# A two-block transformer kernel: the value weights of the dilated attention split over 768 of their 1024 columns, one of their splits issued earlier, and the last two head results read ahead of the keys

## The reference, cut to what matters

```python
proj = h @ w_in                       # 3*768 attention columns, then RWKV-7 streams and gates
y_attn = dilated_attention(proj[..., :2304], positions) @ attn_w_up   # 12 heads of 64, 3 dilations
y_rwkv = rwkv7_time_mix(token_shift(proj[..., 2304:...], mu), ...)
merged = gates[..., :D] * y_attn + gates[..., D:] * y_rwkv
```

## Time and profile before

| what | value |
|---|---|
| runs | 1980.54, 1982.11, 1982.14 us |
| the profiled execution, its own time | 1982.24 us |
| its span in the trace | 1980.4 us |
| PE, ACT, DVE, POOL busy | 96%, 57%, 59%, 39% |
| chain that ended last | 90% PE, 5% DVE, 3% ACT, 1% POOL |

### The profile page before, as it was taken

One profiled execution on the slowest core, in us unless ns is written; L12 is line 12 of the kernel. 1 busy time (PEld: TensorE's weight loads), 2 busy tenths in 40 slices (PEclk: granted clock), 3 DMA queues, 4 the chain that ended last, 5 costly groups with the idle time before them and its releaser, 6 DMA issues.

```text
span 1980.4 us, 33174 instructions
## 1 busy us (share of the span) xinstructions
PE 1909.9 (96%) x12988; PEld 1649.7 (83%) x12988; DVE 1162.0 (59%) x1595; ACT 1133.7 (57%) x1532; POOL 779.5 (39%) x348
## 2 busy tenths in 40 slices
PE   7999989999999999999999999999989899999997
PEld 7999878888987899989787888888878788888885
DVE  2222474766553222264124888888864688888886
ACT  4344556444454544443454777777754467777775
POOL 6888686520068788867772000000057300000000
PEclk9999999999999999999999999999999999999999
DMA  6555443310035555445446998888644579889882
GB/s 233 185 189 186 149 143 138 107 66 3 3 108 186 191 191 190 175 144 192 149 169 260 345 346 341 337 339 340 254 150 158 194 300 343 336 339 345 335 338 98
DMA packets 59315, 425.70 MB, mean 215 GB/s; under 512 B 6577, under 2 KB 7089, under 8 KB 8113
## 3 DMA queue, kind: packets, MB, share of 16 engines
q1 hardware_dynamic: 58032, 419.02, 56.7%
q10 hardware_dynamic: 1152, 4.85, 0.7%
HBM read 422.79 MB, written 1.05 MB: 214 GB/s over the span
## 4 chain that ended last, share of the span: by engine, by line
PE 90%; DVE 5%; ACT 3%; issue 1%; POOL 1%; DMA 0%; SPq 0%; ACTq 0%; DVEq 0%; POOLq 0%
PE ps L735 22%; PE ps L761 19%; PE ps L1319 11%; PE ps L1278 7%; PE ps L1280 7%; PE ps L1279 7%; PE ps L1014 7%; PE ps L1266 2%; PE ps L1333 2%; POOL w_low L692 1%; PE ps L1301 1%; ACT w_high L1507 1%; PE ps L923 1%; PE ps L836 0%; ACT arena L1531 0%
## 5 line engine op out<-in xcount | busy, mean ns | idle before, releaser
L692 POOL TENSOR_TENSOR w_low<-ring,w_high 128x1024 fp32r<-128x1024 f32 x312 | 768.8, 2474 | 671.7 <-ACT w_high L1507 670.8
L1507 ACT ACTIVATE w_high<-ring 128x1024 fp32r<-128x1024 f32 x480 | 504.0, 1060 | 465.5 <-PE ps L761 204.3
L2479 DVE TENSOR_TENSOR w_low<-arena,w_high 128x1024 fp32r<-128x1024 f32 x312 | 373.3, 1222 | 48.7 <-ACT w_high L1507 45.5
L735 PE MATMUL ps<-x_high,w_high 128*128 128x256 f32 x1272 | 365.7, 287 | 6.5 <-DVE x_low L2005 5.1
L1507 ACT ACTIVATE w_high<-arena 128x1024 fp32r<-128x1024 f32 x312 | 323.6, 1059 | 66.0 <-PE ps L1280 49.3
L735 PE MATMUL ps<-x_low,w_high 128*128 128x256 f32 x1272 | 359.8, 283 | 0.0
L735 PE MATMUL ps<-x_high,w_low 128*128 128x256 f32 x1272 | 359.8, 283 | 0.0
L1278 PE MATMUL ps<-w_high,x_high 128*128 128x512 f32 x640 | 256.7, 401 | 3.3 <-DVE x_low L2561 2.8
L735 PEld LDWEIGHTS ps<-x_high,w_high 128*128 128x128 f32 x1272 | 243.8, 192 | 10.7 <-issue 7.9
L1280 PE MATMUL ps<-w_high,x_low 128*128 128x512 f32 x640 | 249.6, 390 | 0.0
L1279 PE MATMUL ps<-w_low,x_high 128*128 128x512 f32 x640 | 248.9, 389 | 0.0
(11 more groups left out here) (312 smaller groups left out, 2361.5 us busy)
## 6 DMA issues: line engine op xcount, KB each, us to landing
ring<-in_stream SPq DMA_DIRECT2D x240, 1024.0 KB, 4.8
arena<-in_stream SPq DMA_DIRECT2D x156, 1024.0 KB, 5.3
arena<-in_gains ACTq DMA_DIRECT2D x4, 512.0 KB, 4.0
con<-in_consts ACTq DMA_DIRECT2D x1, 1280.0 KB, 7.3
con<-in_consts SPq DMA_DIRECT2D x1, 1248.0 KB, 13.8
x<-in_x SPq DMA_DIRECT2D x2, 512.0 KB, 4.0
arena<-in_gate_bias ACTq DMA_DIRECT2D x1, 1024.0 KB, 4.3
out_dram<-arena SPq DMA_DIRECT2D x2, 512.0 KB, 2.6
```

What stands on the lines that cost most here:

```text
L692: nc.gpsimd.tensor_tensor(w_low[:, t % AHEAD, :], slot(SLOT[t // 2])[:, t % 2 * TW:t % 2 * TW + TW], w_high[:, t % AHEAD, :].bitcast(F32), ...
L735: mm = pe.matmul(dst, wp[rows, t % AHEAD, w], xp[rows, x0 + k, :], start=(k == 0 and n == 0), stop=(k == k_tiles - 1 and n == 2))
L1507: nc.scalar.activation(w_high[:, t % AHEAD, :], slot(SLOT[c])[:, t % 2 * TW:t % 2 * TW + TW], ACT.Copy)\
L2479: nc.vector.tensor_tensor(w_low[:, t % AHEAD, :], slot(SLOT[c])[:, t % 2 * TW:t % 2 * TW + TW], w_high[:, t % AHEAD, :].bitcast(F32), ALU. ...
```

## The change

Three edits. First, `columns(t)` gives 768 for the tiles 84 to 91 and 1024 for all others; ACT's split and POOL's subtraction use it, so that the zero padding of the value tiles isn't split. POOL's loop has one width per turn, so its turns 1 to 9 become a loop of six turns, twelve tiles written out (84 to 95, the first eight narrow), and a loop of two turns. Second, the split of tile 87 is issued on ACT after two of the eight key instructions at L1640 instead of after all eight. Third, in the steps 8 and 9 DVE's `evacuate` stands ahead of `keys`, no longer last.

```diff
+        def columns(t):
+
+            return AQ if 2 * START["dil_v"] <= t < 2 * START["dil_v"] + 8 else TW
...
@@ POOL, low(t, turn) @@
-                nc.gpsimd.tensor_tensor(w_low[:, t % AHEAD, :], slot(SLOT[t // 2])[:, t % 2 * TW:t % 2 * TW + TW],
-                                        w_high[:, t % AHEAD, :].bitcast(F32), ALU.subtract).then_inc(w_low_ready, 1)
+                w = columns(t) if turn is None else TW
+                nc.gpsimd.tensor_tensor(w_low[:, t % AHEAD, 0:w], slot(SLOT[t // 2])[:, t % 2 * TW:t % 2 * TW + w],
+                                        w_high[:, t % AHEAD, 0:w].bitcast(F32), ALU.subtract).then_inc(w_low_ready, 1)
...
-            with pool.Fori(1, before_solve) as i:
+            narrow = 2 * START["dil_v"] // 12
+            assert narrow * 12 == 2 * START["dil_v"]
+            with pool.Fori(1, narrow) as i:
+                for t in range(12):
+                    low(t, i)
+            for t in range(narrow * 12, narrow * 12 + 12):
+                low(t)
+            with pool.Fori(narrow + 1, before_solve) as i:
                 for t in range(12):
                     low(t, i)
...
@@ ACT, split(t, turn) @@
-                nc.scalar.activation(w_high[:, t % AHEAD, :], slot(SLOT[c])[:, t % 2 * TW:t % 2 * TW + TW], ACT.Copy)\
+                w = columns(t)
+                nc.scalar.activation(w_high[:, t % AHEAD, 0:w], slot(SLOT[c])[:, t % 2 * TW:t % 2 * TW + w], ACT.Copy)\
                     .then_inc(w_high_ready, 1)
...
@@ ACT, the key instructions at L1640 @@
                     if p == 2:
                         used(t0 + 18)
+                        split_to(t0 + 18 + AHEAD)
...
@@ DVE, the steps n @@
+                    if n >= 8 and n <= 9:
+                        evacuate(n - 2)
                     if n == 5:
                         inverse()
                     if 6 <= n <= 9:
                         keys(n - 6)
                     if n < 8:
                         normalised(n)
-                    if 2 <= n <= 9:
+                    if 2 <= n <= 7:
                         evacuate(n - 2)
```

## The result

The changed kernel takes 1980.9 us (median of 20 runs, 1974.5 to 1985.3) against 1985.3 us for the kernel before (20 runs, 1980.0 to 1992.4): ratio 0.9977, 95% interval 0.9966 to 0.9987, so 4.4 us faster, between 2.6 and 6.7. Forecast were 1975.0 us, in a range of 1972.8 to 1978.4, and 7.2 us of gain. The direction is right. The forecast is 5.9 us too low: by 3.1 because the kernel before is slower than its first three runs said (1982.1, now 1985.3), and by 2.8 because the gain is smaller.

What follows compares the result with a forecast made beforehand. PE, busy 96% of the span, was taken as the bound, so only its idle or low-clock time could be won. 4.5 + 3.6 - 0.1 = 8.0 us, or 6.5 with one fall; 7.2 taken, giving 1975.0 us, range 1972.8 to 1978.4.

Steps and rivals of the forecast that it cites:

- The narrow split: Value tiles 84 to 91: POOL's subtraction 1.82 us for 2.37, scores 4.5 us earlier, 1.5 of it from the clock.
- The early split: ACT's split of tile 87 issued earlier: costed at nothing, bounds 0 to 0.3 us gained, no loss.
- POOL's cut loop: POOL's loop cut in three, seams before tile 84 and at tile 96: taken as 0.
- The head results ahead of the keys: Steps 8 and 9: 2.25 us of PE idle and 1.34 of lower clock saved, 3.6 us.
- The give-back in step 10: L2114's second half might meet a POOL tile, costing PE up to 0.5 us; taken as 0.1.
- The price of the clock: PE's falls to about half clock after idle stretches: each costs about 1.5 us; none or one would remain.
- The level: Starting time of the kernel before: profiled execution 1982.24 us, median 1982.11, so 1982.2 was taken.
- POOL's tile 86 ahead of the sum: Value tiles: POOL's tile 86 starts before DVE's running sum; 1974.7 us, or 1976.2 with a fall; 25%.
- the first rival: Only part arrives: the clock falls twice as before but elsewhere; 5.0 us gained, 1977.1 us; 14%.
- The chances: Odds against a 0.2% (4 us) line: faster 0.84, same 0.13, slower 0.03.

Runs made afterwards that it cites:

- the waits filled: The kernel before with matmuls whose results nobody reads added in PE's three idle stretches; ratios 0.9998 and 1.0001 against the kernel before.
- the fourth measurement: The changed kernel without the early split of tile 87, counted as one more measurement of the same work; ratio 0.9967 (0.9953 to 0.9981) against the kernel before.

## Why the prediction was wrong, point by point

- *The narrow split.* Right. 1.82 us a tile, and 0.85 for ACT's split (0.83 said). From the first value tile to tile 86 it gained 0.5 us, as said (and 0.2 before it), from there to tile 90 2.2 (2.3 said), and from tile 90 to the scores the 1.5 us of the fall, in this pair of profiles.
- *The early split and POOL's cut loop.* Right at nothing: 126.3 us with and without the one, and no gap at either seam.
- *The head results ahead of the keys.* Right: `widen(3)` ended at 375.5 and PE lost 0.2 us there. PE reaches unit 7's result 2.3 us sooner. The give-back in step 10 was put at 0.1 us with a bound of 0.5; it is 0.5, by the mechanism named. The reason given for the low end, "since it met none before", says nothing of the new place: the edit moves that instruction (L2114, now L2128), and the prediction has no time for POOL's tile there.
- *The price of the clock: the term that failed in the gain.* "After 0.7 us of idle PE I expect no fall of the clock, so 1.5 us more" and "1.34 (2.79 - 1.45) of the lower clock" took both falls of one execution as a property of the kernel (and the second is 1.3: at full clock the head result takes 1.50 us). Of the 7.2 us forecast, 2.0 were clock (2.8 if no fall stays, 1.3 if one does) and 5.2 work. The work came: 130.9 - 126.3 = 4.6 us, plus 0.2 ahead of the stretch, so 4.8, and what lacks is the 0.5 us in step 10 that was put at 0.1. The clock didn't: three profiles show the stretch at 133.6, 130.9 and 132.5 us, and 130.9 with the waits filled, so on average 1.4 us and not 2.8. A fall that stands where another engine paces PE costs little or nothing. Work and clock by the profiles make 6.2 us; the runs say 4.8 within 1.4, or 5.2 within 1.3 with the fourth measurement. Whether the last 1 us is chance stays open.
- *The level: the larger error in the time.* "The profiled execution took 1982.24 us ...; the median is 1982.11, so the two stand together." They did, but three runs within 1.6 us of one another came from the fast end of a spread of 12 us. That was bad luck, and three runs couldn't show it. The median of 20 is 1985.3. The range allowed "0.8 for the spread of the runs".
- *The rivals.* POOL's tile 86 ahead of the sum didn't happen, by 0.01 us in the profile after, and in no other profile of the changed kernel (POOL's subtraction takes 6.00 us in all, and PE's first wait is 2.5 us). So near a tie, that it didn't happen is luck as much as reckoning. Of the rest, the first rival had the right size, 5.0 us, and half the reason: less won from the clock. It had the falls only move, which two of the three profiles of the changed kernel don't show: they have none before 400 us.
- *The chances.* The gain lies at the line of 0.2%: 0.23%, with 0.13 to 0.34. 0.84 for clearly faster was too sure.

## What to carry to other kernels

Split a gain read from one profile into work that is no longer waited for and time at the lower clock. The first came again in each profile here, to 0.1 us where the clock stayed up; the second is worth only its average over executions, and little or nothing where another engine paces PE. Take the level and its spread from many runs, since three that agree can all be from one end.

When two engines shut each other out for whole instructions, an edit that moves one instruction by 0.6 us can push another one behind 2.4 us of the other engine: lay both timelines side by side at the new times, and where they meet within 0.3 us, count the loss.

## What the runs showed of the hardware

PE's time at half clock differed from 18.9 to 45.1 us between executions of the same kernel (three profiles of the kernel before), and cost 0.345 us for each us (20 runs of the changed kernel). Each of the three waits of the kernel before (3.0, 2.0 and 2.25 us) had a fall behind it in some of its three profiles and none in others. In all the profiles the single stretches of PE idle with a fall right behind them were of 1.6 to 3.0 us; falls also stood behind several shorter ones, as at 266 us behind 1.2 and 0.6 us. Beside a running sum over 2048 columns, POOL's subtraction of 768 columns took 6.00 us for 1.82.
